# Hybrid decoder trunk: the attention output as three products of high and low parts

## The reference

```
proj = a @ w_in[l]                                        # pool, conv, q, k, v, gates
scores = einsum('bhtd,bhsd,bhtsd->bhts', q, k, decay)     # causal, decay = exp(b_t - b_s)
o      = einsum('bhts,bhse->bhte', scores, v)             # plus the carried state of chunks
o = o * rsqrt(mean(o*o) + eps) * norm_g * silu(out_gate)
mix = concatenate([y_pool, y_conv, o]) @ w_out[l]
h = h + RMSNorm_post(mix)
```

## Time and profile before

| | us |
|---|---|
| median of 3 runs | 1012.62 (1012.48 to 1013.42) |
| the profiled execution's own time | 1012.74 |
| its span in the trace | 1010.9 |
| TensorE busy | 1000.7 (99%) |
| VectorE busy | 628.7 (62%) |
| ScalarE busy | 499.3 (49%) |
| GpSimd busy | 260.9 (26%) |

### The profile page before, as it was taken

One profiled execution on the slowest core, in us unless ns is written; L12 is line 12 of the kernel. 1 busy time (PEld: TensorE's weight loads), 2 busy tenths in 40 slices (PEclk: granted clock), 3 DMA queues, 4 the chain that ended last, 5 costly groups with the idle time before them and its releaser, 6 DMA issues.

```text
span 1010.9 us, 21327 instructions
## 1 busy us (share of the span) xinstructions
PE 1000.7 (99%) x8904; PEld 977.8 (97%) x8904; DVE 628.7 (62%) x643; ACT 499.3 (49%) x564; POOL 260.9 (26%) x180
## 2 busy tenths in 40 slices
PE   9999999999999999999999999999999999999997
PEld 8999999999999999999999999999999999999885
DVE  5764453588967745554477455444889787555485
ACT  6554434566566543343555443435675665434331
POOL 0343330113401333330103333301125014333200
PEclk9999999999999999999999999999999999999999
DMA  9765545645454755335747654357454547666521
GB/s 313 224 223 166 167 132 184 216 128 165 128 172 148 237 178 166 130 116 188 230 132 230 188 166 130 114 191 231 127 168 127 176 143 250 189 189 202 188 85 42
DMA packets 164019, 173.87 MB, mean 172 GB/s; under 512 B 9454, under 2 KB 151014, under 8 KB 163958
## 3 DMA queue, kind: packets, MB, share of 16 engines
q1 hardware_dynamic: 162044, 171.28, 53.5%
q10 hardware_dynamic: 1914, 1.72, 0.7%
HBM read 171.91 MB, written 1.06 MB: 171 GB/s over the span
## 4 chain that ended last, share of the span: by engine, by line
PE 96%; DVE 1%; ACT 1%; DMA 1%; SPq 0%; issue 0%; ACTq 0%; POOL 0%; DVEq 0%; POOLq 0%
PE ps L1486 25%; PE ps L1488 25%; PE ps L1487 25%; PE ps L1518 2%; PE ps L1503 2%; PE ps L1519 2%; PE ps L1691 2%; PE ps L1690 2%; PE ps L1692 2%; PE ps L1624 2%; PE ps L1662 2%; PE ps L1663 2%; PE ps L1818 1%; DMA raw<-in_ffn_wu 1%; PE ps L1545 1%; DVE w_lo L904 0%
## 5 line engine op out<-in xcount | busy, mean ns | idle before, releaser
L904 DVE TENSOR_TENSOR w_lo<-raw,w_hi 128x2048 fp32r<-128x2048 f32 (+2 forms) x174 | 383.9, 2211 | 268.9 <-ACT w_hi L588 268.4
L1486 PE MATMUL ps<-x_hi,w_hi 128*128 128x272 f32 (+2 forms) x1608 | 461.9, 287 | 0.5 <-DVE w_lo L904 0.5
L1488 PE MATMUL ps<-x_hi,w_lo 128*128 128x272 f32 (+2 forms) x1608 | 460.3, 286 | 0.0
L1487 PE MATMUL ps<-x_lo,w_hi 128*128 128x272 f32 (+2 forms) x1584 | 453.1, 286 | 0.0
L588 ACT ACTIVATE w_hi<-raw 128x2048 fp32r<-128x2048 f32 (+2 forms) x174 | 310.9, 1790 | 200.3 <-PE ps L1488 138.9
L1486 PEld LDWEIGHTS ps<-x_hi,w_hi 128*128 128x128 f32 x1608 | 302.8, 188 | 3.2 <-DVE w_lo L904 1.0
L1488 PEld LDWEIGHTS ps<-x_hi,w_lo 128*128 128x128 f32 x1608 | 302.3, 188 | 0.0
L1487 PEld LDWEIGHTS ps<-x_lo,w_hi 128*128 128x128 f32 x1584 | 298.2, 188 | 0.0
L1400 POOL TENSOR_TENSOR up<-gate,up 128x544 f32<-128x544 f32 (+1 forms) x44 | 59.4, 1350 | 310.6 <-ACT gate L723 310.6
L1403 POOL TENSOR_TENSOR hid_lo<-up,hid_hi 128x544 f32 (+3 forms) x44 | 122.7, 2789 | 46.0 <-ACT hid_hi L727 46.0
L723 ACT ACTIVATE gate<-gate 128x544 f32<-128x544 f32 (+1 forms) x44 | 28.7, 653 | 197.1 <-DVE gate L1120 197.1
(11 more groups left out here) (237 smaller groups left out, 1105.3 us busy)
## 6 DMA issues: line engine op xcount, KB each, us to landing
raw<-in_ffn_wg SPq DMA_DIRECT2D x87, 512.0 KB, 4.0
raw<-in_ffn_wu SPq DMA_DIRECT2D x87, 512.0 KB, 4.9
raw<-in_ffn_wd SPq DMA_DIRECT2D x72, 384.0 KB, 3.2
raw<-in_w_in SPq DMA_DIRECT2D x40, 512.0 KB, 4.5
raw<-in_ffn_wd SPq DMA_DIRECT2D x20, 512.0 KB, 4.7
raw<-in_ffn_wd SPq DMA_DIRECT2D x28, 256.0 KB, 3.2
raw<-in_w_out SPq DMA_DIRECT2D x12, 512.0 KB, 5.1
raw<-in_w_out SPq DMA_DIRECT2D x8, 256.0 KB, 4.4
```

The lines of the kernel that those rows point to most:

```text
L904: v_.tensor_tensor(w_lo[:, slot, 0:n], raw[:, slot, 0:n], f32(w_hi[:, slot, 0:n]), ALU.subtract)\
L1486: pe.matmul(out_, wh, xh, start=first, stop=False)
L1487: pe.matmul(out_, wh, xl, start=False, stop=False)
L1488: return pe.matmul(out_, wl, xh, start=False, stop=last)
```

## The change

The attention output becomes three `float32r` products of high and low parts, as the products with weights already are. `v_tok` becomes `v_hi` with `v_lo` and `v_end_lo`, `s_all` becomes `s_hi` with `s_lo`, and `s_last` gets `s_last_hi`, `s_last_lo`. The low parts are written by VectorE. GpSimd clears `s_lo` once more, after the last job, since it lies over `qd_more`. ScalarE copies job 5 before job 4 (`OUT_ORDER`), and `ahead(11)` moves behind the squares of the output. `yq_hi`, `yq_lo`, `v_lo`, `v_end_lo`, `v_end` lie over tiles that are no longer needed at that time (not shown).

```diff
+OUT_ORDER = (MASKED + 1, MASKED, MASKED + 2, MASKED + 3)
...
                     for ch in range(2):
-                        act.activation(v_tok[:, ch, :], ps[:, ch, :], ACT.Copy)
-                    act.activation(v_tok[:, 2, 0:P], ps[:, 6, 0:P], ACT.Copy).then_inc(vt_out, 1)
+                        act.activation(v_hi[:, ch, :], ps[:, ch, :], ACT.Copy).then_inc(vt_out, 1)
+                    act.activation(v_hi[:, 2, 0:P], ps[:, 6, 0:P], ACT.Copy).then_inc(vt_out, 1)
...
-                    for j in range(MASKED, JOBS):
+                    for j in OUT_ORDER:
                         scores_out(j)
+                    act.activation(s_last_hi[:, :, :], s_last[:, :, :], ACT.Copy).then_inc(act_out, 1)
                     load_table(ACT.Sqrt)
                     for a in range(2):
                         act.wait_ge(y_ready, 6 * m + a + 1)
                         high_y(yq_hi[:, 2 + a, t1:T], c_cu[:, a, t1:T])
-                    ahead(11)
                     for p_ in range(2):
                         act.wait_ge(o_mm, 2 * m + p_ + 1)
                         act.activation(o_sq2[:, p_, :, t1:T], ps[:, 4 + 2 * p_:6 + 2 * p_, t1:T], ACT.Square)\
                            .then_inc(o_sq, 1)
+                    ahead(11)
...
                     take_scores(0)
                     k_decay(2)
+                    for ch in range(2):
+                        v_.wait_ge(vt_out, 3 * m + ch + 1)
+                        v_.tensor_tensor(v_lo[:, ch, :], ps[:, ch, :], f32(v_hi[:, ch, :]), ALU.subtract)
+                    v_.wait_ge(vt_out, 3 * m + 3)
+                    v_.tensor_tensor(v_end_lo[:, :], ps[:, 6, 0:P], f32(v_hi[:, 2, 0:P]), ALU.subtract).then_inc(v_low, 1)
...
+                    v_.wait_ge(s_cleared, m + 1)
+                    v_.wait_ge(act_out, 6 * m + 1)
+                    for o in range(0, P, 32):
+                        v_.tensor_tensor(score_block(s_lo, o), s_c[o:o + 32], f32(score_block(s_hi, o)), ALU.subtract)
+                    for n, j in enumerate(OUT_ORDER):
+                        v_.wait_ge(act_out, 6 * m + (2 if n == 0 else 5))
+                        for (dst, src), (hi, _) in zip(score_pieces(s_lo, j), score_pieces(s_hi, j)):
+                            last = v_.tensor_tensor(dst, src, f32(hi), ALU.subtract)
+                    last.then_inc(s_low, 1)
+                    v_.wait_ge(act_out, 6 * m + 6)
+                    v_.tensor_tensor(s_last_lo[:, :, :], s_last[:, :, :], f32(s_last_hi[:, :, :]), ALU.subtract).then_inc(s_end, 1)
...
+                    pool.wait_ge(job_mm, JOBS * (m + 1))
+                    pool.memset(f32(s_lo.rearrange("p c h t -> p (c h) t")[:, :, 0:P]), 0.0).then_inc(s_cleared, 1)
...
-                    pe.wait_ge(vt_out, m + 1)
+                    pe.wait_ge(v_low, m + 1)
                     part("cb", 0, 0, 4)
...
                     act_has(5)
+                    pe.wait_ge(s_low, m + 1)
                     for hh in range(HEADS):
-                        vv = v_tok[:, :, hh * P:(hh + 1) * P]
+                        of_head = slice(hh * P, (hh + 1) * P)
                         o = ps[:, 4 + hh]
-                        pe.matmul(o[:, t1:T], vv[:, 0], s_all[:, 0, hh, t1:T], start=True, stop=False)
-                        pe.matmul(o[:, P:T], vv[:, 1], s_all[:, 1, hh, 0:P + TAIL], start=False, stop=False)
+                        for vv, s_, first in ((v_hi, s_hi, True), (v_lo, s_hi, False), (v_hi, s_lo, False)):
+                            pe.matmul(o[:, t1:T], vv[:, 0, of_head], s_[:, 0, hh, t1:T], start=first, stop=False)
+                            pe.matmul(o[:, P:T], vv[:, 1, of_head], s_[:, 1, hh, 0:P + TAIL], start=False, stop=False)
+                    pe.wait_ge(s_end, m + 1)
                     for hh in range(HEADS):
 
                         rows_ = slice(32 * hh, 32 * hh + 32)
-                        last = pe.matmul(ps[:, 4 + hh, 2 * P:T], v_tok[rows_, 2, 0:P], s_last[rows_, hh % 2],
-                                         start=False, stop=True)
+                        o = ps[:, 4 + hh, 2 * P:T]
+                        pe.matmul(o, v_hi[rows_, 2, 0:P], s_last_hi[rows_, hh % 2], start=False, stop=False)
+                        pe.matmul(o, v_end_lo[rows_, :], s_last_hi[rows_, hh % 2], start=False, stop=False)
+                        last = pe.matmul(o, v_hi[rows_, 2, 0:P], s_last_lo[rows_, hh % 2], start=False, stop=True)
```

More of the change, by code:

```diff
@@ L201, in trunk @@
         laid[0] = 0
+        q_at = arena_at + laid[0]
         q = place("q", [P, 2, T])
         k = place("k", [P, 2, T])
+        v_at = arena_at + laid[0]
         v = place("v", [P, 4, T])
         b = place("b", [P, 2, T])
+        la_at = arena_at + laid[0]
         la = place("la", [P, 2, T])
@@ L208, in trunk @@
         dec = place("dec", [P, 2, 2, T])
+        qd_at = arena_at + laid[0]
         qd = place("qd", [P, 2, 2, T])
         kd = place("kd", [P, 2, 2, T])
-        v_tok = place("v_tok", [P, 3, 512])
-        s_all = place("s_all", [P, 2, HEADS, T])
+        v_end_at = arena_at + laid[0] + 4 * (2 * 512 + P)
+        v_hi = place("v_hi", [P, 3, 512], F32R)
+        s_hi = place("s_hi", [P, 2, HEADS, T], F32R)
         s_c = place("s_c", [P, 2, 4, 32])
         s_last = place("s_last", [P, 2, TAIL])
+        s_last_hi = place("s_last_hi", [P, 2, TAIL], F32R)
+        s_last_lo = place("s_last_lo", [P, 2, TAIL], F32R)
         g_out = place("g_out", [P, 4, T])
@@ L217, in trunk @@
         more_at = arena_at + laid[0]
-        yq_hi = place("yq_hi", [P, 4, T], F32R)
-        yq_lo = place("yq_lo", [P, 4, T], F32R)
+        s_lo = place("s_lo", [P, 2, HEADS, T], F32R)
+        yq_hi = nc.alloc_sbuf_tensor_at("yq_hi", [P, 4, T], F32R, offset=qd_at)
+        yq_lo = nc.alloc_sbuf_tensor_at("yq_lo", [P, 4, T], F32R, offset=q_at)
+        v_lo = nc.alloc_sbuf_tensor_at("v_lo", [P, 2, 512], F32R, offset=v_at)
+        v_end_lo = nc.alloc_sbuf_tensor_at("v_end_lo", [P, P], F32R, offset=la_at)
         mid = place("mid", [P, 2, T // BASE])
@@ L226, in trunk @@
         r_sq = g_out[:, 3, :]
-        v_end = v_tok[:, 2, P:2 * P]
+        v_end = nc.alloc_sbuf_tensor_at("v_end", [P, P], F32, offset=v_end_at)[:, :]
         inv_dec = lt
@@ L348, in trunk @@
         vt_out = sem("vt_out")
+        v_low = sem("v_low")
+        s_cleared = sem("s_cleared")
+        s_low = sem("s_low")
+        s_end = sem("s_end")
         block = ctx.enter_context(nc.Block())
@@ L440, in job_col, with score_block, score_pieces @@
             return 0 if j < MASKED + 1 else P if j < JOBS - 1 else P + 2 * LATE
+        def score_block(of, o):
+            return of[o:o + 32, :, :, o:o + 32].rearrange("p c (a r) t -> p r (c a) t", r=2)
+        def score_pieces(of, j):
+            bank, c0 = job_bank(j), job_col(j)
+            if j < JOBS - 2:
+                bs = 2 * BASE << (j - 1)
+                hf = bs // 2
+                return [(of[o:o + hf, :, :, o + hf:o + bs].rearrange("p c (a r) t -> p r (c a) t", r=2),
+                         ps[o:o + hf, bank:bank + 2, c0:c0 + 4 * hf].rearrange("p r (g t) -> p r g t", g=4))
+                        for o in range(0, P, bs)]
+            c, n = (0, LATE) if j == JOBS - 2 else (1, TAIL)
+            return [(of[:, c, :, P:P + n].rearrange("p (a r) t -> p r a t", r=2),
+                     ps[:, bank:bank + 2, c0:c0 + 2 * n].rearrange("p r (a t) -> p r a t", a=2))]
         def factors(two, more, j):
@@ L776, in scores_out @@
                         act.wait_ge(job_mm, JOBS * (m + 1))
[L777 to L789, removed]
+                        for dst, src in score_pieces(s_hi, j):
+                            last = act.activation(dst, src, ACT.Copy)
                         last.then_inc(act_out, 1)
@@ L837, in _ @@
                     for o in range(0, P, 32):
-                        last = act.activation(s_all[o:o + 32, :, :, o:o + 32].rearrange("p c (a r) t -> p r (c a) t", r=2),
-                                              s_c[o:o + 32], ACT.Copy)
+                        last = act.activation(score_block(s_hi, o), s_c[o:o + 32], ACT.Copy)
                     last.then_inc(act_out, 1)
-                    for j in range(MASKED, JOBS):
+                    for j in OUT_ORDER:
                         scores_out(j)
+                    act.activation(s_last_hi[:, :, :], s_last[:, :, :], ACT.Copy).then_inc(act_out, 1)
                     load_table(ACT.Sqrt)
@@ L1418, in _ @@
                     pool.memset(s_last[:, :, :], 0.0)
-                    pool.memset(s_all.rearrange("p c h t -> p (c h) t")[:, :, 0:P], 0.0)
+                    pool.memset(f32(s_hi.rearrange("p c h t -> p (c h) t")[:, :, 0:P]), 0.0)
                     pool.memset(z_pad[:, :, 0:2], 0.0)
@@ L1804, in act_has @@
                     def act_has(n):
-                        pe.wait_ge(act_out, 5 * m + n)
+                        pe.wait_ge(act_out, 6 * m + n)
                     def job(j):
```

## The result

The changed kernel takes 1022.63 us (median of 5 runs, 1021.74 to 1024.01) against 1013.01 (1012.48 to 1013.42) for the kernel before: a ratio of 1.0095, 95% interval 1.0085 to 1.0106. It is slower, by 9.6 us. The prediction was 1014.3 with a range up to 1017.6; the time lies outside it.

A forecast was written before the change was run, and what follows sets the result against it. TensorE's own list and new waits were taken to bound the kernel. Heads 0.02 + 0.06 and short products 2 x 0.77 gave +1.6 us, the scale chain 0.1: +1.7, so 1014.3 us, range 1012.4 to 1017.6.

The forecast's parts named there:

- What bounds the kernel: Whole kernel: TensorE holds 96% of the last chain; only its own list or a new wait can move the time.
- Products of the heads: TensorE, attention output: wide product 0.125 us, narrow 0.11 by its weight load; heads change by +0.02 and +0.06 us.
- the sign that I named: TensorE's timeline, if right: starts of a narrow product and the next wide one 0.11 us apart.
- float32 price: Rival, attention output: each narrow product costs 0.24 us in place of 0.11, +3.1 us, 1017.4 in all; chance 0.20.
- loads hidden: Rival, attention output: narrow products cost only their columns, 0.066 us; 1013.2 in all; chance 0.15.
- Short products: TensorE, 16-column products of the heads: eight load steps of 0.11 us in place of one, +0.77 us a layer.
- Low parts of values and scores: VectorE's low parts come before TensorE wants them, spare 0.5 us for values, 2.5 and 1.3 for scores; cost nothing.
- The late `low_unit(11)`: VectorE, attention output: it ends at 285.6, the reciprocal follows 1.45 us later than before; priced 0.1 us for both layers.
- the idle 3.80 us: VectorE's gap ahead of the reciprocal, said to absorb the 3.3 us by which the convolution's first step moves.
- The third rival: Chain of `ahead(11)` and the reciprocal, or `v_low`, is 0.5 us a layer worse; 1015.3 in all; chance 0.12.

The follow-up runs named there:

- e4_narrow16: The changed kernel with its narrow products cut to their last 16 columns, output incomplete: 1021.56 us in one run.
- e5_both: The changed kernel with unit 15's transfer held until the scales are back and `ahead(11)` ahead of the squares again: 1014.27 us, ratio 1.0012.
- e3_only_unit11: The kernel before with only `ahead(11)` moved behind the squares: 1018.52 us, ratio 1.005.
- e2_unit11_back: The changed kernel with `ahead(11)` ahead of the squares again: 1022.1 us, ratio 1.0084.
- e1_load_held: The changed kernel with the transfer of weight unit 15 held until the output's scales are back from memory: 1014.7 us, ratio 1.001.
- e6_before_load_late: The kernel before with unit 15's transfer held until the reciprocal is done, so issued together with the scales' write: 1017.33 us, ratio 1.0039.
- e7_mixed: The changed kernel with unit 15's transfer held, `ahead(11)` back, and only the wide products in three float32r parts: 1013.18 us, ratio 1.0002.

## Why the prediction was wrong

- **What bounds the kernel:** right. TensorE's list and new waits are all that count.
- **Products of the heads:** right. A pair takes 0.24 us (277.22 to 277.46), as 0.125 + 0.11. The starts inside a pair lie 0.17 and 0.07 apart (277.22, 277.39, 277.46), so the sign that I named, 0.11 from a narrow product to the next wide one, can't be read; only the pair can. e4_narrow16 shows that the narrow product doesn't cost its columns. The rivals on the narrow products (float32 price; loads hidden) fall.
- **Short products:** mis-sized, +0.1 us a layer in place of +0.77. The trace has them four by four: four L1943 on four groups of rows, then four L1944, four L1945, in steps of 0.11 to 0.14. The order on record has three in a row on one group; I took that for the order in which the array gets them. It was two steps in place of one, not eight in place of one. "Strictly as they are written", which I say of the engines where I describe the kernel, isn't what TensorE's rows show here.
- **Low parts of values and scores:** TensorE never waits for `s_low` or `v_low`, as predicted; `z_pad` starts at 274.88 where I had 274.2. "Cost nothing" is wrong all the same. In the second layer `z_pad` starts 5.0 us late (782.38 in e5_both against 777.34), more than the 3.28 us of idle time ahead of the reciprocal, and the reciprocal comes at 791.56 against 789.89, 1.1 us more than TensorE itself is behind. I had worked this out for the first layer only. And in both layers `low_unit(11)` is late by it, see the next point.
- **The late `low_unit(11)`, by the moved `ahead(11)` and by the low parts:** this is the step that failed. Its time was right (reciprocal 285.67, predicted 285.6), its price wrong: "I price it at 0.1 us for both layers together, from 0 to 1.0." It came to 2.7 + 3.2 us of waits and 3.1 us of half clock. I followed what waits for the reciprocal but not what `low_unit(11)` itself releases: the buffer of unit 15, and with it 1 MB on the same 16 DMA engines in front of a 4 KB write that lies on the path. I also took the write at its old length. The move is enough for this by itself (e3_only_unit11), and so is the backlog of the low parts (e2_unit11_back), which I took to be absorbed by the idle 3.80 us. The third rival, "a wait takes over", named the chain and priced it at 0.5 us a layer; the waits alone are six times that.
- **The clock:** no term of the sum held it. That a wait of 2 to 3 us can be followed by 3.6 to 4.7 us at about half speed wasn't in the trace of before, where TensorE never stops so long.

Undone on the chip: hold the transfer (e1_load_held), and 7.9 of 9.6 us are back; make it alone (e6_before_load_late), and 4.2 us are lost. What the change would cost without the collision is e5_both, +1.1 us (+0.12%, 0.03 to 0.21). That is near the predicted +1.7, but by luck, since the terms are others: 0.1 a layer of TensorE's list, and for the rest a late chain in the second layer, where VectorE's backlog delays the reciprocal and a transfer of instructions lies beside the write. That this transfer lengthens the write is only seen together, sixteen times of sixteen; no run took it away alone.

## What to carry to other kernels

When a step is moved, follow also the buffer that it frees: the transfer that starts then may run into a small one on the critical path, and here 512 KB issued in the same moment as a 4 KB write more than doubled it (4.0 us against 1.7). A load with much slack is best released by the end of the delicate transfer, not by the free buffer. Follow it also when the engine is late for another reason: undoing the move alone brought the median back by 0.5 us of 9.6. A stall of TensorE of over 2 us may cost up to twice its length, for the half clock behind it, and not in each execution.

## What the hardware showed that I had not expected

- A 4 KB write that takes 1.7 us alone took 3.9 to 4.1 us with 512 KB issued in the same moment, 4.2 to 4.8 with 1 MB ahead, and 5.0 to 5.7 with 1 MB and a transfer of instructions.
- The half clock doesn't follow each long wait. Of five waits of TensorE of over 2 us, four had it behind them: 2.3 and 3.05 in the changed kernel, 2.35 in e6_before_load_late, 2.7 in e4_narrow16. The longest, 3.1 us in e2_unit11_back, had none, and neither had those of up to 2.0 us in e3_only_unit11.
- float32r products of 144 and of 16 columns cost the same in a pair with a wide one (0.24 us both); twelve wide ones in a row go at 0.125 each (1.50 us in e7_mixed).
